# Fourteen conditioning vectors summed on VectorE during feed-forward and odd mixer, and four broadcasts behind the turn of the mixed rows

## The reference

```python
c_act = jax.nn.silu(c)
for layer in range(2):
    mod = c_act @ cond_w[layer] + cond_b[layer]          # 1024 x 6144 weights, f32
    sh_m, sc_m, g_m, sh_f, sc_f, g_f = split(mod, 6)     # six vectors of 1024
    h = x * (1 + sc_m) + sh_m
    y = even_mixer(h) if layer == 0 else retention_mixer(h)
    x = layer_norm(ALPHA * x + g_m * y)
    h = x * (1 + sc_f) + sh_f
    y = swiglu(h) if layer == 0 else moe_swiglu(h)       # top 2 of 8 experts
    x = layer_norm(ALPHA * x + g_f * y)
```

## Time and profile before

| | |
|---|---|
| time, median of 3 runs | 1742.43 us (1740.64 to 1743.49) |
| the profiled execution: time, span | 1742.85 us, 1740.9 us |
| PE busy | 1617.3 us (93%) |
| DVE busy | 1282.3 us (74%) |
| ACT busy | 1009.3 us (58%) |
| POOL busy | 132.8 us (8%) |
| moved by DMA | 515.33 MB, mean 296 GB/s |
| loads of conditioning weights | 24 of 2048 KB, median 9.1 us from issue to landing |

### The profile page before, as it was taken

One profiled execution on the slowest core, in us unless ns is written; L12 is line 12 of the kernel. 1 busy time (PEld: TensorE's weight loads), 2 busy tenths in 40 slices (PEclk: granted clock), 3 DMA queues, 4 the chain that ended last, 5 costly groups with the idle time before them and its releaser, 6 DMA issues.

```text
span 1740.9 us, 20082 instructions
## 1 busy us (share of the span) xinstructions
PE 1617.3 (93%) x7810; PEld 1297.4 (75%) x7810; DVE 1282.3 (74%) x1160; ACT 1009.3 (58%) x867; POOL 132.8 (8%) x94
## 2 busy tenths in 40 slices
PE   4888996999969999879999999999999999999996
PEld 1874765787858777658888888888888888888875
DVE  1374536655456665688889888898898898988986
ACT  1432223444434444347777777777777777777775
POOL 0421310000000100220000000000000000000005
PEclk8898998999989999979999999999999999999998
DMA  9347885855454543539999999999999999999993
GB/s 329 130 167 283 322 316 193 285 183 185 169 169 146 164 171 145 187 129 391 388 379 390 375 388 387 369 388 379 376 389 375 381 388 371 384 385 367 385 382 151
DMA packets 234370, 515.33 MB, mean 296 GB/s; under 512 B 8936, under 2 KB 40960, under 8 KB 234176
## 3 DMA queue, kind: packets, MB, share of 16 engines
q1 hardware_dynamic: 228272, 491.99, 77.3%
q10 hardware_dynamic: 2992, 11.79, 1.9%
q0 software_dynamic: 3008, 10.20, 1.9%
HBM read 507.15 MB, written 13.11 MB: 299 GB/s over the span
## 4 chain that ended last, share of the span: by engine, by line
PE 86%; DVE 7%; issue 2%; ACT 2%; DMA 2%; POOL 1%; DVEq 0%; SPq 0%; ACTq 0%; POOLq 0%
PE bank L762 25%; PE bank L764 25%; PE bank L763 25%; PE bank L741 2%; PE bank L925 2%; DMA ring<-in_cond_w 2%; PE bank L1185 1%; PE bank L757 1%; DVE arena L1768 1%; DVE small L1689 1%; PE bank L774 0%; ACT w_part L1310 0%; DVE w_part L1643 0%; DVE hs L1715 0%; PE bank L1167 0%
## 5 line engine op out<-in xcount | busy, mean ns | idle before, releaser
L1654 DVE TENSOR_TENSOR w_lo<-ring,w_hi 128x2048 fp32r<-128x2048 f32 x336 | 764.7, 2290 | 104.1 <-ACT w_hi L1537 102.2
L1537 ACT ACTIVATE w_hi<-ring 128x2048 fp32r<-128x2048 f32 x334 | 640.5, 1918 | 196.3 <-PE bank L764 187.0
L762 PE MATMUL bank<-w_lo,heT_hi 128*128 128x512 f32 x896 | 353.8, 395 | 3.8 <-DVE w_lo L1654 2.2
L764 PE MATMUL bank<-w_hi,heT_hi 128*128 128x512 f32 x896 | 349.7, 390 | 0.0
L763 PE MATMUL bank<-w_hi,heT_lo 128*128 128x512 f32 x896 | 348.9, 389 | 0.0
L1643 DVE TENSOR_TENSOR w_part<-ring,w_part 128x1024 fp32r<-128x1024 f32 x148 | 183.4, 1246 | 211.0 <-ACT w_part L1310 206.2
L1310 ACT ACTIVATE w_part<-ring 128x1024 fp32r<-128x1024 f32 (+1 forms) x162 | 169.1, 1049 | 252.0 <-PE bank L764 247.3
L762 PEld LDWEIGHTS bank<-w_lo,heT_hi 128*128 128x128 f32 x896 | 168.3, 188 | 39.0 <-issue 5.9
L764 PEld LDWEIGHTS bank<-w_hi,heT_hi 128*128 128x128 f32 x896 | 168.2, 188 | 35.9
L763 PEld LDWEIGHTS bank<-w_hi,heT_lo 128*128 128x128 f32 x896 | 168.5, 188 | 33.6
L762 PE MATMUL bank<-w_part,hT_hi 128*128 128x512 f32 (+1 forms) x448 | 179.8, 401 | 14.2 <-DVE w_part L1643 13.1
(11 more groups left out here) (344 smaller groups left out, 1586.8 us busy)
## 6 DMA issues: line engine op xcount, KB each, us to landing
ring<-in_moe_w_up SPq DMA_DIRECT2D x224, 1024.0 KB, 8.8
ring<-in_moe_w_down SPq DMA_DIRECT2D x112, 1024.0 KB, 7.8
ring<-in_cond_w SPq DMA_DIRECT2D x24, 2048.0 KB, 9.1
ring<-in_ffn_w_up SPq DMA_DIRECT2D x22, 1024.0 KB, 8.2
ring<-in_od_w_in SPq DMA_DIRECT2D x8, 2048.0 KB, 7.9
ring<-in_ev_w_in SPq DMA_DIRECT2D x5, 2048.0 KB, 12.4
ring<-in_ffn_w_down SPq DMA_DIRECT2D x5, 2048.0 KB, 7.7
ring<-in_od_w_in SPq DMA_DIRECT2D x8, 1024.0 KB, 8.0
```

Of the source, the lines that this page charges most:

```text
L762: mm(bank, lhs[0], rhs[1], start=start, stop=False)
L764: return mm(bank, lhs[0], rhs[0], start=False, stop=stop)
L1537: f(w_hi[:, n % 3], half_landed(act, it, u, half), ACT.Copy) \
L1654: tt(w_lo[:, buf], at, w_hi[:, buf].bitcast(F32), ALU.subtract).then_inc(S["w_lo"], 1)
```

## The change

`COND_BATCHES` loses its third batch and the end of its second: ten of the 24 units stay with TensorE's row products. The other fourteen (`SUM_COND`) are placed in the stream of feed-forward and odd mixer, one behind each of fourteen units (`SUM_AT`), mostly every third place. VectorE sums each into `acc`: one instruction for the bias, eight that multiply 128 x 512 weights with a scalar of `c_act` per partition and add (`sum_cond`). One step follows each split of a part, two that of part 3. A sum begins with the first unit behind its load. The slot of such a unit is free when its sum is done (`summed`). TensorE then sums over the partitions and broadcasts with one product with ones; `SPREAD_AT` places it. The broadcasts of units 6 to 9 of layer 0, till now behind levels 3 and 4, stand behind the turn of the mixed rows. `cT`, the column of `c_act`, is kept; a tile `sum_bias` is zeroed and loaded on GpSimd; the DMA scratch is made smaller. At the very end the affine step of row block 0 goes from GpSimd to VectorE.

```diff
-COND_BATCHES = (tuple((0, u) for u in FIRST_COND), tuple((0, u) for u in range(4, N_COND)),
-                tuple((1, u) for u in range(N_COND)))
+COND_BATCHES = (tuple((0, u) for u in FIRST_COND), tuple((0, u) for u in range(4, 10)))
+SUM_COND = ((0, 10), (0, 11)) + tuple((1, u) for u in range(N_COND))
...
-LEVEL_COND = {2: (4, 5), 3: (6, 7), 4: (8, 9)}
...
+LEVEL_COND = {2: (4, 5)}
+MIX_COND = (6, 7, 8, 9)
+SUM_AT = {
+    ("ffn_up", 1): 0, ("ffn_up", 3): 1, ("ffn_up", 5): 2, ("ffn_up", 7): 3, ("ffn_up", 9): 4,
+    ("ffn_down", 0): 5, ("ffn_down", 2): 6, ("ffn_down", 4): 7,
+    ("od_v", 0): 8, ("od_qk", 1): 9, ("od_g", 1): 10, ("od_v", 2): 11, ("od_qk", 3): 12, ("od_g", 3): 13,
+}
+SPREAD_AT = {
+    ("ffn_up", 4): (0,), ("ffn_up", 6): (1,), ("ffn_up", 8): (2,), ("ffn_up", 10): (3,),
+    ("ffn_down", 2): (4,), ("ffn_down", 4): (5,),
+    ("od_qk", 0): (6,), ("od_g", 0): (7,), ("od_v", 1): (8,), ("od_qk", 2): (9,), ("od_g", 2): (10,), ("od_v", 3): (11,),
+    ("router",): (12, 13),
+}
...
+    for key, n in SUM_AT.items():
+        order.insert(order.index(key) + 1, ("cond", *SUM_COND[n]))
...
         def slot_read(eng, key):
 
-            if key[0] == "cond":
+            if key[0] == "cond" and key[1:] in SUM_COND:
+                eng.wait_ge(S["summed"], SUM_COND.index(key[1:]) + 1)
+            elif key[0] == "cond":
                 eng.wait_ge(S["cond_used"], cond_order.index(key[1:]) + 1)
...
             def cond(l, u):
 
                 bank, full = to_fill(pe, "cond", l, u)
+                if (l, u) in SUM_COND:
+                    n = SUM_COND.index((l, u))
+                    pe.wait_ge(S["summed"], n + 1)
+                    mm(bank[:], ones, acc[:, n % 2], start=True, stop=True).then_inc(full, 1)
+                    return
...
                     tt(part_buffer(key, 1), slot_part(dve, key), part_buffer(key, 0).bitcast(F32),
                        ALU.subtract).then_inc(S["w_lo"], 1)
+                    sum_cond(key, 2 if key[-1] == 3 or key[:-1] == ("ffn_down", 5) else 1)
...
+            def sum_cond(key, steps):
+
+                for _ in range(steps):
+                    n, k = sums[0] // (KC + 1), sums[0] % (KC + 1) - 1
+                    if n == len(SUM_COND) or stream_place["cond", *SUM_COND[n]] > stream_place[key[:-1]]:
+                        return
+                    sums[0] += 1
+                    l, u = SUM_COND[n]
+                    total = acc[:, n % 2]
+                    if k < 0:
+                        filled(dve, "cond", *(SUM_COND[n - 2] if n > 1 else (0, 9)))
+                        dve.wait_ge(S["sum_bias_in"], 16)
+                        col = N_COND * l + u
+                        V.do(ts(total, sum_bias[:], ident[:, col:col + 1], None, ALU.mult))
+                        continue
+                    _, w = weights(dve, "cond", l, u)
+                    V.wait()
+                    last = stt(total, w[:, 512 * k:512 * k + 512], cT[:, k:k + 1], total, ALU.mult, ALU.add)
+                    if k < KC - 1:
+                        V.do(last)
+                    else:
+                        last.then_inc(S["summed"], 1)
...
-    nc = bacc.Bacc("TRN2", target_bir_lowering=False, num_devices=1)
+    nc = bacc.Bacc("TRN2", target_bir_lowering=False, num_devices=1, dynamic_dma_scratch_size=4096)
```

More of the change, by code:

```diff
@@ L139, in stream_units @@
     e = lambda *n: [("ev_in", i) for i in n]
-    order = c(0, *FIRST_COND) + e(0, 1, 2, 5, 4, 3) + c(0, *range(4, N_COND)) + c(1, *range(N_COND))
+    order = c(0, *FIRST_COND) + e(0, 1, 2, 5, 4, 3) + c(0, *range(4, 10))
     order += [("ev_out", 0), ("ev_out", 1)]
@@ L183, in pe_order @@
         o += ([("ws", n)] if n else []) + ([("kv", n)] if n < 3 else [])
-    o += [("go", t) for t in range(NT)] + [("cond_rows", 2)]
-    o += [("hT", 1, i) for i in (2, 3, 0, 1)]
+    o += [("go", t) for t in range(NT)]
+    o += [("hT", 1, i) for i in (2, 3, 0, 1)] + [("cond", 0, u) for u in MIX_COND]
     o += [("ev_out", u, t) for u in range(2) for t in range(NT)]
@@ L188, in pe_order @@
     for u in range(FFN // 256):
-        o += [("ffn_up", u, t) for t in range(NT)] + ([("cond", *UP_COND[u - 1])] if u - 1 in UP_COND else [])
+        o += [("ffn_up", u, t) for t in range(NT)] + [("cond", *k) for k in spread_at("ffn_up", u)]
         o += [("ffn_T", u - 1)] if u else []
     o += [("ffn_down", t, h) for t in range(NT) for h in range(2)] + [("ffn_T", FFN // 256 - 1)]
-    o += [("cond", *key) for key in DOWN_COND.values()]
+    o += [("cond", *k) for i in range(6) for k in spread_at("ffn_down", i)]
     o += [("hT", 3, i) for i in BY_TILE]
     for h in range(RH):
-        o += [("od_qk", h, t) for t in range(NT)]
+        o += [("od_qk", h, t) for t in range(NT)] + [("cond", *k) for k in spread_at("od_qk", h)]
         if h:
-            o += [("cond", 1, OD_COND[h - 1])] if h - 1 in OD_COND else []
             o += [("ret_y", h - 1, t) for t in range(NT)]
-        o += [("od_v", h, t) for t in range(NT)] + [("ret_T", h, t) for t in range(NT)]
-        o += [("od_g", h, t) for t in range(NT)] + [("ret_s", h)]
+        o += [("od_v", h, t) for t in range(NT)] + [("cond", *k) for k in spread_at("od_v", h)]
+        o += [("ret_T", h, t) for t in range(NT)]
+        o += [("od_g", h, t) for t in range(NT)] + [("cond", *k) for k in spread_at("od_g", h)] + [("ret_s", h)]
         if h:
@@ L205, in pe_order @@
     o += [("hT", 4, i) for i in BY_TILE]
-    o += [("routerT",), ("router",), ("rank",)]
+    o += [("routerT",), ("router",)] + [("cond", *k) for k in spread_at("router")] + [("rank",)]
     o += [("rows_T", 0), ("rows_T", 1)]
@@ L758, in cond, with spread @@
                     .then_inc(full, 1)
+            def spread(*key):
+                for l, u in spread_at(*key):
+                    cond(l, u)
             def three(bank, lhs, rhs, start, stop):
@@ L1116, in _ @@
                 project(("od_v", h), 3)
+                spread("od_v", h)
                 for t in range(NT):
@@ L1124, in _ @@
                 project(("od_g", h), 3)
+                spread("od_g", h)
                 for t in range(NT):
@@ L1149, in _ @@
             narrow("router", logit_rows)
+            spread("router")
             pe.wait_ge(S["late_in"], 16)
@@ L1427, in _ @@
             turned(1, (2, 3, 0, 1))
-            cond_kept(2)
             split_to(part_no["ev_out", 0, 0] + BUFS)
+            for u in MIX_COND:
+                cond(0, u)
             for u in range(2):
@@ L2201, in _ @@
             to_normalise(3, 1)
+            affine(3, 0)
             affine(3, 1)
```

61 lines of the change are left out of this document (28 added, 33 removed).

## The result

The changed kernel took 1922.97 us (median of four runs, 1919.9 to 1926.2) against 1742.96 us for the one before: a ratio of 1.104, with a 95% interval of 1.101 to 1.106. The forecast was 1902 us with a range of 1850 to 1935. The profiled execution took 1926.2 us, with a span of 1924.4 us, 183.5 us more than the 1740.9 of before. It is the slowest of the four, so readings from its trace stand some 3 us above the median.

The account below looks back on a forecast made before the run. TensorE was taken to bound feed-forward and odd mixer while split weights lie ready. Gains of -23.5 us and waits of +183.2 (87.2 + 61.5 + 9 + 25.5) on 1742.85 gave 1902 us, range 1850 to 1935.

Parts of the forecast that it names:

- What bounds the stages: Feed-forward and odd mixer: set by TensorE alone, which stays fed only as long as split weights lie ready.
- T + 19.8: Weights behind a conditioning load ready 19.8 us after TensorE reads part 0 (T); it stands still from T + 8.6.
- The clock: Behind each of fifteen waits TensorE restarts at a lower clock: 1.7 us each, 25.5 us (bounds 0 and 30).
- VectorE's steps: 126 added instructions at 0.684 us, 86 us: nothing in the feed-forward; 9 us in the odd mixer through late od_v.
- The even mixer: Fourteen units of rows and four broadcasts leave its chain: stage ends 22.8 us earlier (bounds 15 and 26).
- a lower clock between the short products: Even mixer: one of two reasons given for the lower bound of 15 us on its 22.8 us gain.
- The four broadcasts behind the turn: Even mixer: removal between levels gains 3.8 us; behind the turn, mostly covered by TensorE's idle time, +1 (0 to 3.5).
- Small ones: Two broadcasts behind the router +0.5 us; row block 0's affine on VectorE at the end -0.5; scratch, bias tile, DMA 0.
- no waits: Rival 2: only the 23.5 us gained in the even mixer show, 1719 us; chance 0.05.
- shorter waits: Rival 1: loads land in 13.3 us, clock stays up, engines hide 1 us at each wait: 1854 us; chance 0.14.
- VectorE becomes the bound: Rival 3: a third of VectorE's added 86 us come on the path, 1902 + 29 = 1931 us; chance 0.13.
- The even mixer's gain fails: Rival 4: without fillers TensorE runs short products at 1.2 GHz, the 22.8 us become about 0: 1925 us; chance 0.05.

Follow-up runs that it names:

- three-step kernel: Changed kernel with three steps of a sum behind each split part instead of one (two behind the last part), all loads and instructions kept: 1766.68 us, ratio 1.014.
- first kernel with busy waits: Changed kernel with 34 to 50 small products of no use on TensorE ahead of ten of the fifteen late units: 1918.54 us, ratio 1.101.

## Why the prediction held, point by point

- **What bounds the stages.** Right: TensorE alone bounded feed-forward and odd mixer, and the lead of the split weights was the question. The loss lies there: 197.5 us, with 15.2 gained ahead of them and 1.2 lost behind.
- **The waits on SyncE's queue (T + 19.8).** Right, in mechanism and size. In the wait shown above TensorE stands still for 11.0 us; 11.2 was forecast. The second of the two loads landed 13.5 us after its issue and 13.9 after the first's; 14.0 had been taken, between the 14.7 of the earlier trace rows and the 13.3 added up from the earlier trace rows. The eight waits of the feed-forward are 9.9, 11.0, 11.5, 11.1, 11.0, 10.0, 11.8 and 9.4 us, 85.7 in all (87.2 forecast). Those of the odd mixer are 8.5, 11.3, 9.7, 12.8, 8.9, 11.0 and 7.4, 69.6 in all (61.5). The shorter ones before part 3 are 9.8 us, against 5.7 in the earlier trace rows, so 4.1 more (9). Together 159.4 against 157.7. So near a sum is partly luck: the odd mixer's seven waits were 8.1 us too low together (none by more than 2.3), od_v's shorter ones 4.9 too high. TensorE's idle time as a whole grew by 160.5 us.
- **The clock.** Right in kind, too small: the 3.4 us idle of the earlier trace rows was the nearest row and gave 1.7 us a wait. Here the first part behind an 11 us wait ran wholly at 1.2 GHz, 5.46 instead of 2.72 us: a loss of 2.7 us. That is one of the largest. TensorE was busy at the lower clock for 3.2 to 5.6 us behind each of the fifteen waits, 67.9 us in all; at half speed half of that is lost, so 34 us (2.3 a wait) instead of 25.5. Elsewhere in the two stages, behind od_v's shorter waits and at the starts of stages, the same count gives 4 us more than before. The stages add up: 160.5 of idle time + 37.8 of clock - 1.7 for two fewer broadcasts = 196.6, measured 101.8 + 95.7 = 197.5.
- **VectorE's steps.** "Nothing in the feed-forward" is right: 1.7 us without most of them. In the odd mixer they are worth 9.4 us. That the forecast had 9 us is luck: it had them all as late parts of od_v, and without the steps these waits shrink by only 3.1 us; the rest is spread over the other waits (3.0) and TensorE's busy time (3.3). A step was dearer than its row of 684 ns, 90 us in all instead of 77 for the 112:

```profile
L1701 DVE SCALAR_TENSOR_TENSOR acc<-ring,small,acc 128x512 f32<-128x512 f32 x112 | 89.9, 802 | 1.7
```

  The 802 is a mean; 106 of the steps took 743 to 753 ns, and six took 1.78 us.

- **The even mixer.** Here a step failed: -21.8 us up to the feed-forward were forecast (22.8 less 1), -15.2 came, and the first product of `ev_out` stands at 255.7 us where about 246 was given as a sign. Up to the attention's products 17.8 us are gained (237.5 to 219.8) of 20.5 forecast, and 2.4 of the missing 2.7 are the lower clock at the Y transposes. The row ahead of them was said to be in TensorE's idle time and to bring nothing; it had kept that idle time short. In the three-step kernel, where the clock stayed up, the gain to the same point is 20.5 us. VectorE's lateness, which the forecast saw, costs 0.94 us at level 1 and nothing behind it, so the later levels had room for it as the forecast wrote. Behind the attention 2.6 us were lost where 1.3 were to be gained, and the fillers in the state chain give 3.7 back: they were on the path and at the same time they kept the clock up. The forecast named this ("a lower clock between the short products") as one of two reasons for its lower bound of 15, and put it at nothing in its value; it is 6.1 of the 6.6 us that are missing.
- **The four broadcasts behind the turn.** The forecast had the move between levels and turn as -3.8 and +1. The run that undoes it lost 5 us: 3.4 between the levels and -0.8 behind the turn, both as forecast, and 2.3 in `ev_out`, which begins at the full clock behind the broadcasts. That last term the forecast did not have.
- **Small ones.** The router's two broadcasts +0.8 (forecast +0.5), experts and end +0.4 (-0.5).
- **The whole.** The profiled execution took 1926.2 us where 1902.5 was forecast: 16 us from the two stages (12.3 of the clock, 2.8 of idle time, 0.9 unaccounted), 6.6 from the even mixer, 1.2 from the small ones. Of the rivals, "no waits" and "shorter waits" fall with TensorE's 166.6 us of waits. "VectorE becomes the bound" gave 1931 us, near the result, but for a reason that did not hold: it wanted 29 us from VectorE, and with 28 of the 126 instructions 1912 us remain, 11 less. "The even mixer's gain fails" is a third true.

The Trainium skill, "DMA: Bandwidth & Descriptors", section "Anatomy of one DMA", gives 2.0 us plus the bytes at 436 GB/s for DMAs that GpSimd issues; by it an estimate for both loads is 11.6 us. The 13.9 us here speak against that rule for SyncE's queue, as the rows of before did.

## What to carry to other kernels

Work given to an engine with idle time is free only if the buffers that it holds come free in time: look up what is queued behind the instruction that waits for the buffer, and add up release, queue, landing and split against the moment of need. Spreading such work thinly is what made it dear here: with the same 126 instructions the kernel is 180 us slower than the one before at one step per part, and 25 at three. And before fillers are taken off a chain of short products, ask what they do for the clock, also where they stand in idle time, and what else is late by less than their length. Last, a sum that is near the forecast doesn't show that its terms are right: add up each term from the trace.

## What the runs showed of the hardware that was not expected

- In the first kernel with busy waits, 2.1 us of idle time behind a stretch of small products were followed by a fall of the granted clock, and it came late: 1.00 in the window with the idle time, 0.56 in the next, when TensorE was busy again. Of the ten idle times left there, those of 1.94, 2.08 and 2.20 us were followed by it, the seven of 0.6 to 1.9 us were not.
- The same idle time in the same code does not always lower the clock: of the 2.08 us ahead of the Y transposes seven traces show 0.50 behind it and four 1.00.
- Gaps of 0.8 to 1.3 us between groups of eight products of 1.1 us brought the clock to 0.50 from 230 to 242 us; the same chain with small products in the gaps ran at 1.00:

```profile
230.00:242.00 12.00, 8.71 (x45) 7.86 (x45) 3.62 (x10) 0.00 (x0) 0.00 (x0) 0.50 0.01 2
```

```profile
230.00:242.00 12.00, 11.35 (x109) 10.28 (x109) 4.30 (x11) 0.50 (x1) 0.00 (x0) 1.00 0.17 60
```

- A step of a sum on a 128x512 tile took 747 ns (median) with its weights in the ring, and 746 ns in the run without loads, where it reads `sum_bias`. So reading from the ring doesn't make the difference to the 684 ns on `hs` and `xs`; what does was not tried.
- Six of the 112 steps took 1.78 us. Each of them overlaps an instruction of GpSimd on a tile of the same size, as here:

```profile
531.24 2.15 POOL L2305 TENSOR_TENSOR mod<-ln,mod 128x512 f32<-128x512 f32 x1
532.17 1.78 DVE L1701 SCALAR_TENSOR_TENSOR acc<-ring,small,acc 128x512 f32<-128x512 f32 x1
```
